# A hybrid decoder step: x loaded ahead of the weights, squares added in pairs, S5 products between the norm's steps

## The chip, the cores and the metric

The kernel runs on one core of a Trainium2 chip. The metric is device microseconds of one execution; lower is better. All data are f32.

## What is computed

One decoder layer over a prompt of 1024 tokens and, beside it, one new token for each of 8 decode sequences whose keys and values (8192 positions) lie in a paged cache.

```
hn = rmsnorm(x, ln1_g)                       # x: 1024 prompt rows + 8 decode rows, 1024 wide
q, k, v, u = split(hn @ w_in)                # 512 columns each
attn = differential attention(rope(q), rope(k), v)     # 4 heads x 2 maps; decode rows read 64 pages of 128 each
s5   = gated S5 state-space group(u)         # 32 groups of 16 channels, 64 complex states
x = x + concat(attn, s5) @ w_out
x = x + hier_moe(rmsnorm(x, ln2_g))          # top-1 of 4 groups, top-2 of 8 experts
y = rmsnorm(x, ln_f_g)
```

lam, which weighs the second attention map, comes from four small vectors (`lamv`) by two dot products and two exponentials.

## The kernel before, in words

Each engine runs its own list of units. The order of the units is written by a small planner (`streams`, `make_plan`): every unit has a TensorE cost and a list of units that must precede it with a lag; the planner puts the streams together by rank, and gives each unit its banks of PSUM (6 banks in turn, `banks`). TensorE, VectorE and GpSimd run the same order `PLAN`; ScalarE runs it sorted by the planned ends. The decode stream has the highest rank. Its unit `K` or `V` multiplies 8 pages of the cache; pages come in a ring of 16 (two units), are sent by the sync queue in a fixed order as slots come free, and the planner paces one unit (2.1 MB) each 7.1 us. Below it stand attention (S, C, T, O), the S5 group (`s5a`, b units), and the projections in halves of 4 of the 8 k slices: `u` (S5 columns transposed, four column blocks n by two token halves a, in parts f), then k, v, q.

Ahead of the planned part three units stand fixed: `stats`, `dqkv`, `dprep`.

- Loads: the sync queue sends, for k = 0 to 7, slice k of x (`xm`) and slice k of the four weight blocks (`w_q, w_k, w_v, w_u`), then the first 16 pages. GpSimd's queue sends consts, colw, rope, br, wr, bglu, lamv and the S5 tables par and bc.
- `stats`: ScalarE squares each slice into one of two buffers `sq`; TensorE sums it over the partitions with a matrix of ones (two products of 512 columns and one of 8 for each slice), VectorE scales the slice by ln1_g (L1025). Then VectorE copies the sums to one row (L1027), TensorE turns the row into columns (18 instructions of one column), VectorE adds eps, GpSimd takes the power -1/2 (L553), VectorE builds 8 diagonals of rstd (L1046).
- `dqkv`: TensorE multiplies the 8 decode rows with all four weight blocks, side by side in four column blocks of the array; ScalarE copies the results (L738), VectorE scales and rotates them.
- `dprep`: TensorE spreads rstd over the partitions (`rep`), transposes the decode queries, keys and S5 inputs (12 transposes, L1805); VectorE writes the queries into `qpad` (32 copies), which the K units read, and the keys into `knT`.
- `lam` runs first of all on VectorE (L1008 to L1017), with one exp on ScalarE.

Matmuls are all recorded at line 1764 (a helper), transposes at L1805 and others.

## Time and profile before

| what | value |
|---|---|
| runs | median 1478.14 us, 1476.67 to 1494.74, 3 runs |
| profiled execution | 1475.24 us |
| its span, first to last instruction | 1473.5 us |
| mean granted TensorE clock | 0.938 |
| busy: TensorE, VectorE, ScalarE, GpSimd | 87%, 35%, 17%, 14% |
| DMA | 458.35 MB, mean 311 GB/s |

The profile shows one execution. Times are in us from the start of the span; the time of an execution is 1.7 us longer than the span here. PE is TensorE, DVE VectorE, ACT ScalarE, POOL GpSimd, SP the sync engine; a trailing q is the engine's sequencer. A matmul of f32 appears as two instructions.

### The profile page before, as it was taken

The page shows a single profiled execution, that of the slowest core. Times are in us where ns is not written, and L with a number is a line of the kernel's source. Part 1 is how long each engine was busy: PE and PEld are TensorE (multiplying, and loading weights), DVE is VectorE, ACT ScalarE, POOL GpSimd, SP SyncE. Part 2 cuts the span into 40 slices and gives each one's busy share as a digit, 9 for nine tenths or more (in the row PEclk, how much of TensorE's full clock was granted, in tenths as well). Part 3 has the DMA queues.
Part 4 walks back from the last instruction along what each step waited for, and adds up shares of the span by engine and source line. Part 5 has one row for each costly group of instructions (what it writes and reads, how often), then busy time and mean ns, then how long its engine had stood idle before and what let it go on. Part 6 is the DMA issues. An engine that isn't in the chain of part 4 may idle for free.

```text
span 1473.5 us, 26489 instructions
## 1 busy us (share of the span) xinstructions
PE 1284.7 (87%) x8952; PEld 670.8 (46%) x8952; DVE 522.2 (35%) x1430; ACT 248.1 (17%) x473; POOL 212.9 (14%) x327
## 2 busy tenths in 40 slices
PE   4799899999889878899869999987799999999930
PEld 2455565654334335566654443433344444444410
DVE  1461344443564555455531121134221121112126
ACT  2200111120122222233321000000111111111111
POOL 1101204040401100000010000000112222222121
PEclk9899999999988989999999999986999999999975
DMA  9499979979987987999996998998899999999754
GB/s 355 173 318 317 340 258 304 344 236 319 313 286 250 366 285 251 368 330 312 325 372 253 337 337 294 314 348 309 284 332 363 368 372 360 367 364 373 259 202 186
DMA packets 186454, 458.35 MB, mean 311 GB/s; under 512 B 24177, under 2 KB 24561, under 8 KB 177778
## 3 DMA queue, kind: packets, MB, share of 16 engines
q1 hardware_dynamic: 165906, 394.41, 75.6%
q0 software_dynamic: 20448, 62.59, 12.7%
q8 instruction: 66, 1.08, 0.3%
q14 instruction: 34, 0.28, 0.1%
HBM read 421.92 MB, written 33.80 MB: 309 GB/s over the span
## 4 chain that ended last, share of the span: by engine, by line
PE 71%; DMA 9%; DVE 8%; SPq 5%; issue 3%; DVEq 2%; ACT 1%; POOL 1%; ACTq 0%; POOLq 0%; PEldq 0%
PE WA L1764 53%; PE SC L1764 7%; PE OD L1764 6%; DMA ring<-in_cacheK 3%; SPq L489 3%; DMA ring<-in_cacheV 2%; PE WA L2110 2%; DMA arena<-in_x_s 1%; SPq L477 1%; PE WA L1865 1%; DVE arena L1733 1%; DVE st L1105 1%; DMA ring<-h_scratch,idc 1%; DMA xm<-in_xT 1%; DVE arena L1746 1%
## 5 line engine op out<-in xcount | busy, mean ns | idle before, releaser
L1764 PE MATMUL WA<-arena 128*128 128x512 f32 (+9 forms) x1440 | 351.8, 428 | 15.3 <-issue 7.1
L1764 PE MATMUL WA<-arena,xm 128*128 128x512 f32 (+2 forms) x768 | 315.7, 619 | 8.7 <-DMA arena<-in_w_out 6.6
L1764 PEld LDWEIGHTS WA<-arena 128*128 128x128 f32 (+2 forms) x1440 | 192.6, 195 | 148.6 <-issue 132.6
L1764 PEld LDWEIGHTS WA<-arena,xm 128*128 128x128 f32 (+1 forms) x768 | 123.5, 182 | 164.1 <-issue 155.9
L1764 PE MATMUL WA<-xm,arena 128*128 128x512 f32 x192 | 88.8, 610 | 1.7 <-ACT arena L936 1.3
L553 POOL TENSOR_TENSOR st<-st,consts 128x1 f32<-128x1 f32 (+2 forms) x18 | 13.8, 765 | 465.5 <-DVEq L1139 279.0
L1764 PE MATMUL OD<-ring,sall 128*32 128x512 f32 x512 | 69.8, 660 | 11.9 <-DMA ring<-in_cacheV 11.9
L1764 PE MATMUL OD<-ring,qpad 128*32 128x128 f32 x2048 | 64.1, 275 | 8.9 <-DMA ring<-in_cacheK 8.7
L1764 PE MATMUL SC<-ring,qpad 128*32 128x128 f32 x2048 | 64.4, 276 | 7.7 <-DMA ring<-in_cacheK 7.5
L1676 DVE TENSOR_TENSOR xm<-WA,colw 128x960 f32<-128x960 f32 x16 | 18.5, 1158 | 147.1 <-PE WA L2110 147.1
L1676 DVE TENSOR_TENSOR arena<-WA,colw 128x960 f32<-128x960 f32 x16 | 18.5, 1158 | 137.5 <-PE WA L2110 137.3
L1764 PEld LDWEIGHTS OD<-ring,qpad 128*32 128x32 f32 x2048 | 53.4, 110 | 28.3 <-issue 16.3
L1764 PEld LDWEIGHTS SC<-ring,qpad 128*32 128x32 f32 x2048 | 54.2, 111 | 26.5 <-issue 16.5
L1764 PE MATMUL SC<-ring,sall 128*32 128x512 f32 x512 | 63.9, 619 | 1.7 <-DMA ring<-in_cacheV 1.7
L804 ACT ACTIVATE arena<-WA,st 128x128 f32<-128x128 f32 (+7 forms) x64 | 47.4, 741 | 94.8 <-DVEq L1109 93.7
L1764 PE MATMUL WA<-ring,xm 128*128 128x512 f32 x128 | 57.5, 603 | 0.0
L671 POOL DMA_DIRECT2D y_dec<-arena x32 | 17.8, 557 | 268.8 <-ACT arena L943 268.8
L1764 PE MATMUL WA<-xm 128*128 128x512 f32 x128 | 56.3, 592 | 0.0
L1764 PEld LDWEIGHTS WA<-xm,arena 128*128 128x128 f32 x192 | 35.7, 194 | 42.1 <-issue 40.5
L943 ACT ACTIVATE arena<-WA 128x1024 f32<-128x1024 f32 x32 | 32.8, 1024 | 125.1 <-PE WA L1764 125.1
L1427 DVE TENSOR_TENSOR arena<-arena,WA 128x512 f32<-128x512 f32 x16 | 11.0, 688 | 113.5 <-PE WA L1764 88.4
L1105 DVE TENSOR_REDUCE st<-WA 128x1 f32<-128x128 f32 (+7 forms) x64 | 48.5, 758 | 5.5 <-issue 0.9
(359 smaller groups left out, 1250.0 us busy)
## 6 DMA issues: line engine op xcount, KB each, us to landing
ring<-in_cacheK SPq DMA_DIRECT2D x512, 256.0 KB, 4.7
ring<-in_cacheV SPq DMA_DIRECT2D x512, 256.0 KB, 4.7
arena<-in_w_gu SPq DMA_DIRECT2D x16, 2048.0 KB, 8.6
arena<-in_w_dn SPq DMA_DIRECT2D x16, 1024.0 KB, 12.5
ring<-in_w_gu SPq DMA_DIRECT2D x8, 2048.0 KB, 8.6
xm<-in_w_gu SPq DMA_DIRECT2D x8, 2048.0 KB, 8.6
arena<-in_w_in SPq DMA_DIRECT2D x32, 256.0 KB, 10.2
ring<-in_w_dn SPq DMA_DIRECT2D x8, 1024.0 KB, 12.6
```

The lines of the kernel that those rows point to most:

```text
L477: sp.dma_start(w[:, k, :], io["w_in"][n, k, :, :]).then_inc(s_wk[k], 16)
L489: sp.dma_start(ring[:, GRP * half + j, :], cache[bass.ds(pages[j], 1), :, :] .rearrange("a p n -> p (a n)")).then_inc(s_pg[PARTS * half + ...
L671: gp.dma_start(io["y_dec"][bass.ds(4 * NB * q + NB * v, NB), :], yb[v % 2][CAP:128, :]).then_inc(m_sd[v % 2], 16)
L804: act.activation(P[:, n % 2, c, 0:w], slot("S", i, h, c)[:, 0:w], ACT.Exp, bias=st[:, 4 * (n % 2) + c:4 * (n % 2) + c + 1], scale=HD ** -0 ...
L943: act.activation(yb[v % 2], W[1][:, :], ACT.Copy).then_inc(m_ys, 1)
L1105: dve.reduce_max(st[:, 8 + c:9 + c], S[:, 0:w], AX)
L1676: dve.tensor_tensor(hgT[v % 2][:, :, 0:CAP], (W[0] if src is None else src)[:, :] .rearrange("p (k n) -> p k n", k=KD)[:, :, 0:CAP], colw[ ...
L1733: dve.scalar_tensor_tensor(x1[0:r, i, :], yg[i][c][0:r, :], wts[0:r, c, i:i + 1], x1[0:r, i, :], MUL, ADD)
L1746: dve.scalar_tensor_tensor(x1[0:r, i, :], x1[0:r, i, :], st[0:r, i:i + 1], lnf[0:r, :], MUL, MUL)\
L1764: return pe.matmul(out, lhsT, rhs, start=first, stop=last, **kw)
L1865: last = pe.transpose(slot("AT", i, h)[:, 128 * j:128 * j + 128], P[:, n % 2, 0, 128 * j:128 * j + 128], ident)
L2110: last = pe.transpose((W[0] if out is None else out)[:, 128 * k:128 * k + CAP], hg[v % 2][0:CAP, 128 * k:128 * k + 128], ident[0:CAP, 0:CAP])
```

## The change

The sync queue sends all of x, then the S5 columns w_u, then the query columns w_q, then pages. w_k and w_v go to GpSimd's queue, sent after `qpad` has been written. GpSimd sends only consts, colw and rope at first; lamv, bglu, br, wr, par and bc follow after the norm's power. ScalarE squares into four buffers, VectorE adds them in pairs (`s_pair`), and TensorE sums over the partitions once for each pair. The fixed head of the order is now: stats, first half of u(0,0), `col` (row to columns), its second half, `dq` (decode queries alone, 128 columns in each of four column blocks), `rep`, first half of u(0,1), `dprep` (4 transposes, 8 copies into qpad, and then `lam`). The decode products of k, v and S5 columns (`dkv`) and their transposes (`dk2`) become units of the projection stream, behind u(3,0). VectorE evacuates u(0,0) after `dprep`. `lam_map` finishes lam at `dkv`.

```diff
-        "stats": [(("ss",), 2)], "dqkv": [(("dp",), 1)], "dprep": [(("rep",), 2), (("dqt",), 1)],
+        "stats": [(("ss",), 2)], "dq": [(("dp",), 1)], "dprep": [(("dqt",), 1)], "rep": [(("rep",), 2)],
+        "dkv": [(("dkv",), 1)], "dk2": [(("dkt",), 1)],
...
-                    dec.append((("K", x, t, g, y), 1.95, [(("ov", SPP * x - 1), 0.8)] if x else []))
+                    dec.append((("K", x, t, g, y), 1.95, [(("ov", SPP * x - 1), 0.8)] if x else [(("dprep",), 0.5)]))
...
     for n in range(4):
         for a in range(2):
             proj += [(("u", n, a, f), half, []) for f in range(2)]
+            if (n, a) == (3, 0):
+                proj.append((("dkv",), 7.5, []))
+    proj.append((("dk2",), 0.9, [(("dkv",), 6.0)]))
...
-    s5 = [(("s5a",), 0.0, [])]
+    s5 = [(("s5a",), 0.0, [(("dprep",), 2.0)])]
     for n in range(NQ):
-        x = [(("bY", n - 1, 1), 0)] if n else [(("u", 3, 1, 1), 4.0), (("s5a",), 60.0)]
+        x = [(("bY", n - 1, 1), 0)] if n else [(("u", 3, 1, 1), 4.0), (("dk2",), 3.0), (("s5a",), 60.0)]
...
-    end, free, nxt = {}, [0.0] * BANKS, 0
-    plan, t = [("stats",), ("dqkv",), ("dprep",)], 0.0
-    land, gone, due = [0.0, 0.0], [], 0.0
+    plan, t = [("stats",), ("u", 0, 0, 0), ("col",), ("u", 0, 0, 1), ("dq",), ("rep",), ("u", 0, 1, 0), ("dprep",)], 0.0
+    end, free = {u: t for u in plan}, [3.0] * BANKS
+    nxt = (max(p + n for p, n, _, _ in [banks(plan)[0][("dqt",)]])) % BANKS
+    at["proj"] = 3
+    land, gone, due = [0.0, 2.0], [], 1.0
     kept, never = {}, 1e9
+    b = banks(plan)[0][("u", 0, 1)][0]
+    free[b], kept[("u", 0, 1, 1)] = never, [b]
...
+    u0, turn = PLAN.index(("u", 0, 0, 1)), PLAN.index(("dprep",)) + 1
+    DVE_PLAN = PLAN[:u0] + PLAN[u0 + 1:turn] + [PLAN[u0]] + PLAN[turn:]
...
-        sq = region(0, 2 * TT, "p (s n) -> p s n", s=2)
+        sq = [region(b, TT) for b in (0, TT, 4096, 4096 + TT)]
...
             for k in range(KD):
                 sp.dma_start(xm[:, k, :], io["xT"][k, :, :]).then_inc(s_xk[k], 16)
-                for n, w in enumerate((w_q, w_k, w_v, w_u)):
-                    sp.dma_start(w[:, k, :], io["w_in"][n, k, :, :]).then_inc(s_wk[k], 16)
+            for k in range(KD):
+                sp.dma_start(w_u[:, k, :], io["w_in"][3, k, :, :]).then_inc(s_wk[k], 16)
+            for k in range(KD):
+                sp.dma_start(w_q[:, k, :], io["w_in"][0, k, :, :]).then_inc(s_wq, 16)
...
-            gp.dma_start(br[:, :], io["b_r"].partition_broadcast(128)).then_inc(s_cst, 16)
-            gp.dma_start(wr[:, :, :], io["w_r"]).then_inc(s_cst, 16)
-            gp.dma_start(bglu[:, :], io["b_glu"]).then_inc(s_cst, 16)
-            gp.dma_start(lamv[:, :, :], io["lamv"].partition_broadcast(128)).then_inc(s_lamv, 16)
-            gp.dma_start(par, io["s5_par"]).then_inc(s_ld5, 16)
-            gp.dma_start(bc, io["s5_bc"]).then_inc(s_ld5, 16)
...
             def stats():
                 gp.memset(qpad[:, :, :, :], 0.0).then_inc(s_qbd, 1)
-                gp.wait_ge(s_cst, 96)
+                gp.wait_ge(s_cst, 48)
                 root(rstd[:, :], ("stats",))
+                gp.dma_start(lamv[:, :, :], io["lamv"].partition_broadcast(128)).then_inc(s_lamv, 16)
+                gp.dma_start(bglu[:, :], io["b_glu"]).then_inc(s_lamv, 16)
+                gp.dma_start(br[:, :], io["b_r"].partition_broadcast(128)).then_inc(s_lamv, 16)
+                gp.dma_start(wr[:, :, :], io["w_r"]).then_inc(s_lamv, 16)
+                gp.dma_start(par, io["s5_par"]).then_inc(s_ld5, 16)
+                gp.dma_start(bc, io["s5_bc"]).then_inc(s_ld5, 16)
...
-            def dqkv():
-                gp.wait_ge(s_drope, 1)
+            def dprep():
+                gp.wait_ge(s_qbd, 2)
+                for n, w in enumerate((w_k, w_v)):
+                    gp.dma_start(w, io["w_in"][n + 1, :, :, :].rearrange("k p n -> p k n")).then_inc(s_wkv, 16)
+
+            def dkv():
+                gp.wait_ge(s_drope, 2)
                 gp.dma_start(io["v_s"], dv[:, :]).then_inc(s_dst, 16)
                 gp.dma_start(io["k_s"], qk[0:NB, QKW:2 * QKW]).then_inc(s_dst, 16)
...
+            def dk2():
+                gp.wait_ge(*filled("dkt"))
...
+                gp.wait_ge(s_qbd, 3)
                 gp.dma_start(io["us_scratch"].rearrange("n p b -> p n b"), usT).then_inc(s_dst, 16)
...
             def stats():
                 for k in range(KD):
                     act.wait_ge(s_xk[k], 16)
-                    if k >= 2:
-                        act.wait_ge(s_sqread, k - 1)
-                    act.activation(sq[:, k % 2, :], xm[:, k, :], ACT.Square).then_inc(s_sq, 1)
-
-            def dqkv():
+                    if k >= 4 and k % 2 == 0:
+                        act.wait_ge(s_sqread, k // 2 - 1)
+                    act.activation(sq[k % 4], xm[:, k, :], ACT.Square).then_inc(s_sq, 1)
+
+            def dq():
                 act.wait_ge(*filled("dp"))
-                for n, out in enumerate((qk[0:NB, 0:QKW], qk[0:NB, QKW:2 * QKW], dv[:, :], du)):
-                    act.activation(out, slot("dp")[32 * n:32 * n + NB, 0:QKW], ACT.Copy)
+                for c in range(4):
+                    act.activation(qk[0:NB, 128 * c:128 * c + 128], slot("dp")[32 * c:32 * c + NB, 0:128], ACT.Copy)
                 act.drain().then_inc(free_sem("dp"), 1)
                 act.drain().then_inc(s_dq, 1)
...
+            def dprep():
+                act.wait_ge(s_lam, 1)
+                act.activation(lamt[:, 2:4], lamt[:, 0:2], ACT.Exp).then_inc(s_lam, 1)
+
+            def dkv():
+                act.wait_ge(*filled("dkv"))
+                for n, out in enumerate((qk[0:NB, QKW:2 * QKW], dv[:, :], du)):
+                    act.activation(out, slot("dkv")[32 * n:32 * n + NB, 0:QKW], ACT.Copy)
+                act.drain().then_inc(free_sem("dkv"), 1)
+                act.drain().then_inc(s_dq, 1)
...
-                    act.wait_ge(*filled("dqt"))
+                    act.wait_ge(*filled("dkt"))
...
             def lam():
-                dve.wait_ge(s_lamv, 16)
+                dve.wait_ge(s_lamv, 64)
...
+
+            def lam_map():
                 dve.wait_ge(s_lam, 2)
...
+                dve.scalar_tensor_tensor(wmap[:, 0:SPP, :].rearrange("p y h -> p (y h)"), consts[:, C_M1:C_M1 + SPP * H],
+                                         lamt[:, 7:8], consts[:, C_M0:C_M0 + SPP * H], MUL, ADD)
+                dve.drain()
 
             def stats():
-                lam()
-                dve.wait_ge(s_cst, 96)
+                dve.memset(rstd[:, NT:NT + 1], 1.0)
+                dve.wait_ge(s_cst, 48)
                 for k in range(KD):
                     dve.wait_ge(s_sq, k + 1)
+                    if k % 2:
+                        dve.tensor_tensor(sq[k % 4 - 1], sq[k % 4 - 1], sq[k % 4], ADD).then_inc(s_pair, 1)
                     dve.tensor_scalar(xm[:, k, :], xm[:, k, :], colw[:, k:k + 1], None, MUL).then_inc(s_xg, 1)
                 dve.wait_ge(*filled("ss"))
                 dve.tensor_copy(sumrow[:, 0:SEQ], slot("ss")[0:1, :])
                 dve.tensor_copy(sumrow[:, SEQ:TT], SC[0:1, 0:NB])
...
-                dve.tensor_scalar(bglu[:, :], bglu[:, :], 0.5, None, MUL)
-                dve.memset(logit[:, NT, :], 0.0)
-                dve.memset(st[:, :], 1.0)
...
                 dve.drain().then_inc(s_rstd, 1)
                 for i in range(NT):
                     dve.tensor_scalar(diag[:, i, :], ident, rstd[:, i:i + 1], None, MUL)
                 dve.drain().then_inc(s_rep, 1)
 
-            def dqkv():
+            def dq():
                 dve.wait_ge(s_dq, 1)
-                r = rstd[0:NB, NT:NT + 1]
-                dve.tensor_scalar(qk[0:NB, :], qk[0:NB, :], r, None, MUL)
-                dve.tensor_scalar(dv[:, :], dv[:, :], r, None, MUL)
-                dve.tensor_scalar(du, du, r, None, MUL)
-                dve.drain()
-                rotate(qk[0:NB, :], NB, NT)
+                dve.tensor_scalar(qk[0:NB, 0:QKW], qk[0:NB, 0:QKW], rstd[0:NB, NT:NT + 1], None, MUL)
+                dve.drain()
+                rotate(qk[0:NB, 0:QKW], NB, NT)
                 dve.drain().then_inc(s_drope, 1)
 
             def dprep():
                 dve.wait_ge(s_qbd, 1)
                 dve.wait_ge(*filled("dqt"))
-                src = slot("dqt")[:, 0:2 * H * NB].rearrange("p (a h b) -> p a h b", a=2, h=H)
+                src = slot("dqt")[:, 0:H * NB].rearrange("p (h x y) -> p h x y", h=H, y=SPP)
                 for h in range(H):
                     for c in range(2):
-                        for y in range(SPP):
-                            dve.tensor_copy(qpad[64 * c:64 * c + 64, h, y::SPP, 8 * y + 2 * h + c],
...
+                        dve.tensor_copy(qpad[64 * c:64 * c + 64, h, :, :].rearrange("p (x y) n -> p x (y n)", y=SPP)
+                                        [:, :, 2 * h + c::40], src[64 * c:64 * c + 64, h, :, :])
                 dve.drain().then_inc(free_sem("dqt"), 1)
+                dve.drain().then_inc(s_qbd, 1)
+                lam()
+                dve.tensor_scalar(bglu[:, :], bglu[:, :], 0.5, None, MUL)
+                dve.memset(logit[:, NT, :], 0.0)
+                dve.memset(st[:, :], 1.0)
+                dve.tensor_scalar(colw[:, 2 * KD:2 * KD + 1], colw[:, 2 * KD:2 * KD + 1], 1.0 - LINIT, None, MUL)
+                dve.drain()
...
+            def dkv():
+                lam_map()
+                dve.wait_ge(s_dq, 2)
+                r = rstd[0:NB, NT:NT + 1]
+                dve.tensor_scalar(qk[0:NB, QKW:2 * QKW], qk[0:NB, QKW:2 * QKW], r, None, MUL)
+                dve.tensor_scalar(dv[:, :], dv[:, :], r, None, MUL)
+                dve.tensor_scalar(du, du, r, None, MUL)
+                dve.drain()
+                rotate(qk[0:NB, QKW:2 * QKW], NB, NT)
+                dve.drain().then_inc(s_drope, 1)
+
+            def dk2():
+                dve.wait_ge(*filled("dkt"))
+                dve.tensor_copy(knT[:, :, :], slot("dkt")[:, 0:H * NB].rearrange("p (h b) -> p h b", h=H))
+                dve.tensor_copy(usT, slot("dkt")[:, H * NB:2 * H * NB].rearrange("p (n b) -> p n b", n=4))
+                dve.drain().then_inc(free_sem("dkt"), 1)
                 dve.drain().then_inc(s_qbd, 1)
...
-            for unit in PLAN:
+            for unit in DVE_PLAN:
...
             def stats():
                 pe.nop().then_inc(s_pgfree, RING // QP)
-                pe.wait_ge(s_cst, 96)
-
-                for k in range(KD):
-                    pe.wait_ge(s_sq, k + 1)
+                pe.wait_ge(s_cst, 48)
+
+                for k in range(KD // 2):
+                    pe.wait_ge(s_pair, k + 1)
                     for out, c0, c1 in ((slot("ss")[:, 0:512], 0, 512), (slot("ss")[:, 512:SEQ], 512, SEQ),
                                         (SC[:, 0:NB], SEQ, TT)):
-                        last = mm(out, ones, sq[:, k % 2, c0:c1], k == 0, k == KD - 1)
+                        last = mm(out, ones, sq[2 * (k % 2)][:, c0:c1], k == 0, k == KD // 2 - 1)
                     last.then_inc(s_sqread, 1)
-                pe.wait_ge(s_sqread, KD)
+                pe.wait_ge(s_sqread, KD // 2)
                 pe.nop().then_inc(full_sem("ss"), 1)
 
+            def dq():
+
+                pe.wait_ge(s_wq, 16 * KD)
+                vacant(pe, "dp")
+                for k in range(KD):
+                    for c in range(4):
+                        last = mm(slot("dp")[32 * c:32 * c + NB, 0:128], xm[:, k, SEQ:TT], w_q[:, k, 128 * c:128 * c + 128],
+                                  k == 0, k == KD - 1)
+                last.then_inc(full_sem("dp"), 1)
+
+            def col():
...
-            def dqkv():
-                pe.wait_ge(s_xg, KD)
-                vacant(pe, "dp")
-                for k in range(KD):
-                    pe.wait_ge(s_wk[k], 64)
-                    for n, w in enumerate((w_q, w_k, w_v, w_u)):
-                        last = mm(slot("dp")[32 * n:32 * n + NB, 0:512], xm[:, k, SEQ:TT], w[:, k, :], k == 0, k == KD - 1)
-                last.then_inc(full_sem("dp"), 1)
-
             def dprep():
+                pe.wait_ge(s_drope, 1)
+                vacant(pe, "dqt")
+                for h in range(H):
+                    last = pe.transpose(slot("dqt")[:, NB * h:NB * h + NB], qk[0:NB, 128 * h:128 * h + 128], ident[0:NB, 0:NB])
+                last.then_inc(full_sem("dqt"), 1)
+
+            def rep_():
                 pe.wait_ge(s_rep, 1)
                 vacant(pe, "rep")
                 for i in range(NT):
                     last = mm(slot("rep")[:, 128 * i:128 * i + 128], ones, diag[:, i, :])
...
-                pe.wait_ge(s_drope, 1)
-                vacant(pe, "dqt")
-                for j in range(3 * H):
-                    src = qk[0:NB, 128 * j:128 * j + 128] if j < 2 * H else du[:, 128 * (j - 2 * H):128 * (j - 2 * H) + 128]
-                    last = pe.transpose(slot("dqt")[:, NB * j:NB * j + NB], src, ident[0:NB, 0:NB])
-                last.then_inc(full_sem("dqt"), 1)
+
+            def dkv():
+                pe.wait_ge(s_wkv, 32)
+                vacant(pe, "dkv")
+                for k in range(KD):
+                    for n, w in enumerate((w_k, w_v, w_u)):
+                        last = mm(slot("dkv")[32 * n:32 * n + NB, 0:512], xm[:, k, SEQ:TT], w[:, k, :], k == 0, k == KD - 1)
+                last.then_inc(full_sem("dkv"), 1)
...
                 if f == 0:
                     vacant(pe, "u", n, a)
                 for k in range(4 * f, 4 * f + 4):
+                    if n + a == 0:
+                        pe.wait_ge(s_xg, k + 1)
+                        pe.wait_ge(s_wk[k], 16)
                     last = mm(slot("u", n, a)[:, :], w_u[:, k, 128 * n:128 * n + 128], xm[:, k, 512 * a:512 * a + 512],
                               k == 0, k == KD - 1)
                 if f == 1:
...
             def m1(x):
                 pe.wait_ge(s_evac, 2 * TURNS * (x + 1))
+                if x == 0:
+                    pe.wait_ge(s_qbd, 3)
```

## Rows read from the trace of the kernel before

**Rows 1.** The page's section 4: the chain that ended last, its shares by engine.

```profile
PE 71%; DMA 9%; DVE 8%; SPq 5%; issue 3%; DVEq 2%; ACT 1%; POOL 1%; ACTq 0%; POOLq 0%; PEldq 0%
```

**Rows 2.** DMA issues from 0 to 60 us: number, KB each, median us from issue to landing.

```profile
xm<-in_xT SPq DMA_DIRECT2D x8, 516.0 KB, 10.6
...
arena<-in_lamv POOLq DMA_DIRECT2D x1, 128.0 KB, 7.6
rope<-in_rope POOLq DMA_DIRECT2D x1, 72.0 KB, 5.6
```

**Rows 3.** Windows: busy us (instructions) by engine, then PEclk, DMA share, GB/s.

```profile
0.00:5.00 5.00, 0.00 (x0) 0.00 (x0) 0.00 (x0) 1.28 (x1) 3.77 (x11) 1.00 0.55 190
...
20.00:25.00 5.00, 5.00 (x15) 2.42 (x14) 1.41 (x2) 1.06 (x1) 0.00 (x0) 1.00 1.04 412
...
50.00:60.00 10.00, 5.84 (x56) 3.21 (x45) 3.25 (x9) 3.60 (x6) 0.61 (x2) 0.89 0.02 7
```

**Rows 4.** Timeline, 0 to 41 us: start, us, engine, line, operation, count, idle time before.

```profile
2.78 0.55 POOL L538 DMA_DIRECT2D rope<-in_rope  x1
...
12.58 0.22 DVE L1008 TENSOR_TENSOR arena<-arena 128x64 f32<-128x64 f32 x1 [12.58 <-DMA arena<-in_lamv]
...
14.72 3.75 PE L1764 MATMUL WA<-arena,consts 128*128 128x512 f32 x4 [14.72 <-ACT arena L733]
...
37.66 1.06 ACT L733 ACTIVATE arena<-xm 128x1032 f32<-128x1032 f32 x1 [2.76 <-DMA xm<-in_xT]
38.76 0.76 DVE L1025 TENSOR_SCALAR xm<-xm,colw 128x1032 f32<-128x1032 f32 x1 [3.07 <-ACT arena L733]
...
38.78 1.98 PE L1764 MATMUL WA<-arena,consts 128*128 128x512 f32 x4 [1.72 <-ACT arena L733]
```

**Rows 5.** Timeline, 41 to 73 us: norm, decode projection, first K unit.

```profile
41.01 1.21 DVE L1027 COPY arena<-WA 1x1024 f32<-1x1024 f32 x1 [1.50 <-PEq L1777]
...
42.38 2.06 PE L1764 MATMUL OD<-consts,arena 1*128 1x1 f32 x18 [1.50 <-DVEq L1029]
...
44.37 8.65 PE L1764 MATMUL WA<-arena,xm 128*8 128x512 f32 x64
...
44.89 1.83 POOL L553 TENSOR_TENSOR rstd<-rstd,consts 128x9 f32<-128x9 f32 x1 [37.38 <-DVEq L980]
...
47.15 1.66 DVE L1046 TENSOR_SCALAR arena<-consts,rstd 128x128 f32<-128x128 f32 x8
...
52.95 2.05 PE L1764 MATMUL WA<-arena,consts 128*128 128x128 f32 x16
...
59.16 1.45 PE L1805 MATMUL WA<-consts,arena 8*128 8x8 f32 x12 [4.16 <-DVEq L1057]
...
60.53 5.75 PE L1764 MATMUL WA<-xm,arena 128*128 128x512 f32 x8
...
66.22 1.95 PE L1764 MATMUL SC<-ring,qpad 128*32 128x128 f32 x64
...
68.10 3.70 PE L1764 MATMUL WA<-xm,arena 128*128 128x512 f32 x8
```

**Rows 6.** Groups of VectorE by form: an SBUF addition or product; busy us, mean ns.

```profile
L1223 DVE TENSOR_TENSOR arena<-arena 128x512 f32<-128x512 f32 x8 | 5.5, 692 | 0.6
```

**Rows 7.** DMA issues from 608 to 640 us.

```profile
arena<-in_w_out POOLq DMA_DIRECT2D x1, 2048.0 KB, 10.4
```

**Rows 8.** TensorE's waits from 608 to 640 us: us in total, times, longest us.

```profile
PE SC L1764 <- DMA ring<-in_cacheK: 2.3, 1, 2.3
```

**Rows 9.** TensorE's waits from 66 to 1000 us: us in total, times, longest.

```profile
PE WA L1865 <- DVEq L1123: 15.3, 8, 5.9
PE OD L1764 <- DMA ring<-in_cacheV: 11.2, 7, 3.6
...
PE OD L1764 <- DMA ring<-in_cacheK: 8.7, 6, 3.3
PE SC L1764 <- DMA ring<-in_cacheK: 7.5, 7, 2.3
```

51 lines of the change are left out of this document (24 added, 27 removed).

## The prediction

> **What bounds the kernel now.** I read the page first: TensorE makes up 71% of the chain that ended last, DMA 9%, VectorE 8%, so TensorE is the bound of the whole [rows 1]. From about 66 us on the kernel is a long queue of TensorE work, in a fixed order, with gaps; what it does before that is a start-up. Then I read the timeline of the first 70 us, because the change touches only that stretch. The reader is to see there a chain of five links.
>
> First, x arrives slowly. The sync queue sends each slice of x (516 KB) followed by four slices of w_in (128x512 f32, 256 KB each) [rows 2], 1,540 KB in all, and the transfers run at 412 GB/s with the DMA engines full [rows 3]: 1.577 MB / 412 GB/s = 3.83 us for each of the eight rounds. The last Square on ScalarE begins at 37.66 and its product on TensorE ends near 40.9 [rows 4]. Second, the norm's small steps: VectorE copies the sums at 41.01, TensorE turns them into columns 42.38 to 44.4, GpSimd takes the power from 44.89 to 46.7, VectorE builds the diagonals from 47.15 to 48.8 [rows 5]. Third, TensorE's decode projection of all four column blocks, 8.65 us from 44.37, then the 16 products for `rep` from 52.95 [rows 5]. Fourth, TensorE stands idle from 55.0 to 59.16 until the copies and the rotation are done, then makes 12 transposes [rows 5]. Fifth, the first half of an S5 product takes 5.75 us where a later one takes 3.70: after that idle time the engine ran it at the low clock for the most part. The first K unit begins at 66.22 [rows 5]. Between 50 and 60 us the DMA engines moved only 7 GB/s [rows 3]: the ring was full and nobody took a page.
>
> **The change, part by part.** I set up the new start-up as a timetable from these rows.
>
> (a) Loads. x goes ahead of all weights, and of GpSimd's transfers only consts, colw and rope stay ahead. Up to 15 us the row of before is not clean (many small packets), so I take its first 5 us (190 GB/s, 0.95 MB) as the start [rows 3] and 410 GB/s from there. x needs 8 x 0.528 = 4.22 MB, the tables 0.54, and about 0.5 MB more has moved when a slice counts as landed (an estimate from before: its last Square, at 37.66, against the bytes ahead of it). The last slice lands at 5 + (5.26 - 0.95)/0.41 = 15.5 us, the S5 columns (2.1 MB) at 20.7, the query columns at 25.8, and the 16 first pages by 36. The rope table, which the gate for VectorE and TensorE now waits for, was issued at 2.78 and took 5.6 us: 8.4 [rows 2, 4].
>
> (b) Squares in pairs. ScalarE: 8 of 1.06 us, from 6.5 on. VectorE does two scalings of 0.76 and one added addition of 128x1032 for each pair; an SBUF addition of 128x512 takes 0.69 [rows 6], and its slope of about 1.04 ns for an element gives 1.23. So 2.75 us a pair. TensorE now makes four sets of products in place of eight: 4 x 2 us saved, of which none lay on the path. The first set runs at the low clock, 3.75 us as before, the others take 2.0 to 2.2 [rows 4]. The timetable: addition 0 ends at 10.4; its products end at 14.1; ScalarE's fifth Square waits for that, since there are four buffers, and ends at 15.2; the sixth at 16.3, addition 2 at 17.5; the seventh Square waits for the second set (16.4 to 17.0), the eighth ends at 19.1; addition 3 at 20.4; the last set at 22.6. The x transfer could be 2 us later without moving this. I take 22.6, with 20.5 (no low clock) and 26 (landing as in the mean of before's first 15 us, and another wait on the table) as its ends. Before it was 40.9.
>
> (c) S5 products between the norm's steps. Now TensorE has work in every gap. From 22.7: half S5 product 3.6, columns 2.1, half 3.6, query projection, `rep` 2.05, half 3.6, 4 transposes 0.5, half 3.6 (no bank is needed, so the planner puts it ahead of the first K unit). The query projection has 64 instructions on 128 columns in four column blocks, the shape of a K unit, 1.95 us [rows 5]; at the low clock it would be 3.9. Sum 22.7 + 3.6 + 2.1 + 3.6 + 1.95 + 2.05 + 3.6 + 0.5 + 3.6 = 43.7 us for the first K unit. The side chains fit under it: the sums are copied by 24.2, before TensorE has ended its half at 26.3; the columns end at 28.4, the power and diagonals follow as before (44.4 to 48.8 is 4.4 us) and are ready at 32.8, while `rep` is needed at 34.0; the queries' copies and rotation take at most what all four blocks took (55.0 minus 52.95 is the time of `rep`, so from 52.95 to 59.16, 6.2 us): from 34.0 to 40.2 against a need at 39.6. At worst 0.6 us shows. The 8 copies into qpad in place of 32 lie beneath the last half. If one of these covers fails the price is that chain's own excess, 1 to 3 us, and if the clock falls during the 2.1 us of columns, one half costs up to 5.75 - 3.6 = 2.2 more [rows 5].
>
> (d) Work moved to later. `dkv` is the old decode projection with three blocks side by side in place of four, still eight steps, and a step on 512 columns is a quarter of 3.6 us: 7.2 us. Its 8 transposes are two thirds of the 1.45 us that 12 took [rows 5]. 8.2 us come back into the TensorE queue. Against it, at the first K unit four S5 halves are done, where before it was one: 3 x 3.6 = 10.8. Net 2.6 more in hand.
>
> (e) w_k and w_v move from the sync queue to GpSimd's and load once qpad is ready (41 us), 4.2 MB or 10.2 us of all DMA engines at 410 GB/s. At first the ring is full and they have the engines alone until page slots come free at 45.7; 2.3 MB are left to run beside the pages. The nearest row is the 2,048 KB of w_out: 10.4 us to land, and TensorE then waited 2.3 us for a page [rows 7, 8]. So 0 to 4.6 us for both; I take 1.5, since half has landed before a page can compete and the next units of K come 12 us later. `dkv` is queued behind some 11 halves, near 90 us, so TensorE won't wait for these weights.
>
> (f) Small loads moved: lamv, b_glu, b_r, w_r behind the power (30.7 us). lamv took 7.6 us [rows 2]; the last of the four was issued at 33 and lands near 41. VectorE waits for all four in `lam`, behind the qpad copies; queued behind that wait are the evacuations of the first two S5 products, whose banks TensorE needs at 45.7. ScalarE's exp is queued ahead of its later copies, and waits for `lam` too. Slack 3 to 4 us, cost nothing; if the loads landed 4 us later each further us would be one on TensorE.
>
> The Trainium skill, "DMA: Bandwidth & Descriptors", section on queues, rings and completion order, says that each DMA engine takes turns between queue rows that have work, a packet at a time. Two busy queues would so get half each, and w_out's row (2.1 MB in 10.4 us, 202 GB/s, half of 410) agrees. By the rule alone the 2.3 MB left in (e) would take 11 us, in which pages are slowed to half: they move 2.3 MB where the planner's pace (2.1 MB in 7.1 us) asks 3.3 MB, so 1.0 MB or 3.5 us late, under the slack of about 4 us, and the sum would lose the 1.5.
>
> **Sum.** TensorE's queue stands 66.2 - 43.7 = 22.5 us earlier at the first K unit and is 2.6 us shorter behind it: 25.1. Less 1.5 for pages: 23.6. The profiled execution took 1475.24 (span 1473.5 and 1.7 around it), so 1451.6. The median of the runs shown is 2.9 higher than that execution and the lowest 1.4 higher; I add 1: 1452. From 20.5 and 26 for the start, 0 to 4.6 for pages and 0 to 2.8 for clock and covers, the likeliest case spans 1446 to 1459.
>
> **The rivals.** A: the pages bound it. The gain of the TensorE queue is then cut by the weights that now load beside pages. Before, with the ring full at 66.2, all of w_in was in; after, with the ring full at 43.7, 2.3 MB are still to come when pages start again: 22.5 - 5.7 = 17, so 1459. For it: DMA engines are full in many slices, and waits of TensorE for pages sum to 27 us over 66 to 1000 [rows 9]. Against it: that is a small part of 934 us, so TensorE is the bound and pages only touch it.
>
> B: more comes back. The written order is made anew from other starting values, other banks and one longer stream, and the waits inside the attention stage (15.3 us on one line of VectorE alone) and for pages are matters of which units meet [rows 9]. These sum to 43 us. If a fifth falls away it is 9 us more: 1443. Nothing in the rows says that it does, and a fifth more of them is as possible: 1461.
>
> C, on the other side: the new order bunches K and V units so that the ring of two units runs dry. A wait of that kind was 3.6 us at its longest [rows 9], so seven more of that size take 25 us, the whole gain, and eight end slower than before, at 1480 against 1478. It decides from the point where the page waits double, from 27 to 51 us. Against it: the pace of pages in the planner is not changed.
>
> D: a cover in (f) fails. GpSimd sends lamv's group from 30.7 on, while VectorE works through diagonals, copies and rotations until 41; before, it sent it to an idle VectorE, whose first instruction is at 12.58 [rows 4], so no row here tests the two together. If those loads get going only when VectorE rests, they land at 41 + 7.6 = 48.6, VectorE frees the first S5 bank at 50, and TensorE, which wants it at 45.7, loses 4.3 us: 1456. That w_k and w_v go the same way costs nothing, with 40 us to spare. The Trainium skill, "SBUF — State Buffer" (section on SBUF's two separate sides), has such a rule: a transfer issued from GpSimd can't have its descriptors written while VectorE runs an instruction in a two-port mode. That VectorE is in that mode for only part of the ten us is why I give it little.
>
> **Chances.** Forecast 0.52, A 0.15, B 0.12 for more and 0.10 for less, C 0.03, D 0.08. The range 1441 to 1463 leaves out 0.15 to 0.2. The bound of 2%, about what a measurement of this kernel can tell from no change, lies at 1448.6 against the median of 1478.14: below it is B's better half and the lower edge of the forecast, 0.12 + 0.16 = 0.28. Above 1507.7 there is a part of C, 0.02. The rest, 0.70, is within 2%.
>
> **What would show it.** In the profile after: the last Square near 18 to 19 us; no gap of TensorE over 1 us between 23 and 44 us; the first K unit at 41 to 47; the clock granted at full from 15 us on; idle DMA only between some 36 and 41 us; the decode products of k, v and S5 near 90 us, 7.2 us long. Then each later landmark (first V unit, the routing) should lie 22 to 28 us earlier. I am wrong if landmarks drift apart after 100 us, which would be order or pages, or if the first K unit lies beyond 48, which would be the start-up.

## The result, and the profile after

The changed kernel took 1465.72 us (median of 8 runs, 1459.21 to 1472.42), the kernel before 1480.12 (median of 8 in all, the three shown first among them, 1475.01 to 1494.74). The ratio is 0.9898, 95% interval 0.9871 to 0.9924: 1.0% faster, 15.1 us on 1480.12, between 11.2 and 19.1. The forecast was 1452, its range 1441 to 1463: too low, and the range misses. The profiled execution after took 1465.81 (span 1464.1), its own median; that of before, 1475.24, turned out to lie 4.9 under its median.

The chain that ended last, from the page of the kernel after, answers to [rows 1]:

```profile
PE 70%; DMA 9%; DVE 7%; SPq 5%; issue 3%; DVEq 2%; ACT 1%; POOL 0%; ACTq 0%; POOLq 0%
```

TensorE is still the bound. The timeline of the kernel after (start, length, engine, line, operation, count, idle time before) answers to [rows 4, 5]:

```profile
8.57 0.76 DVE L1059 TENSOR_SCALAR xm<-xm,colw 128x1032 f32<-128x1032 f32 x1 [7.59 <-DMA rope<-in_rope]
...
10.61 3.75 PE L1807 MATMUL WA<-arena,consts 128*128 128x512 f32 x4 [10.61 <-DVE arena L1058]
...
14.69 2.02 ACT L751 ACTIVATE arena<-xm 128x1032 f32<-128x1032 f32 x2 [3.58 <-PE SC L1807]
...
16.91 2.02 ACT L751 ACTIVATE arena<-xm 128x1032 f32<-128x1032 f32 x2 [0.20 <-PE SC L1807]
...
20.51 1.98 PE L1807 MATMUL WA<-arena,consts 128*128 128x512 f32 x4 [0.37 <-DVE arena L1058]
...
22.92 3.67 PE L1807 MATMUL WA<-xm,arena 128*128 128x512 f32 x8 [0.30 <-PE SC L1807]
...
26.52 2.06 PE L1807 MATMUL OD<-consts,arena 1*128 1x1 f32 x18
...
28.51 5.40 PE L1807 MATMUL WA<-xm,arena 128*128 128x512 f32 x8
...
33.84 1.93 PE L1807 MATMUL WA<-arena,xm 128*8 128x128 f32 x64
...
35.70 2.05 PE L1807 MATMUL WA<-arena,consts 128*128 128x128 f32 x16
...
37.59 3.60 PE L1807 MATMUL WA<-xm,arena 128*128 128x512 f32 x8
...
41.12 0.41 PE L1844 MATMUL WA<-consts,arena 8*128 8x8 f32 x4
...
41.46 3.70 PE L1807 MATMUL WA<-xm,arena 128*128 128x512 f32 x8
...
43.51 1.80 POOL L578 DMA_DIRECT2D arena<-in_w_in x2 [9.41 <-DVEq L1090]
...
45.09 1.96 PE L1807 MATMUL SC<-ring,qpad 128*32 128x128 f32 x64
...
60.78 1.08 PE L1807 MATMUL SC<-ring,qpad 128*32 128x128 f32 x32 [1.15 <-DMA ring<-in_cacheK]
66.07 1.94 PE L1807 MATMUL SC<-ring,qpad 128*32 128x128 f32 x32 [4.21 <-DMA ring<-in_cacheK]
67.93 4.53 PE L1807 MATMUL WA<-xm,arena 128*128 128x512 f32 x8
...
81.57 1.63 PE L1807 MATMUL OD<-ring,qpad 128*32 128x128 f32 x52
```

The reader is to see three things. From 22.9 to 45 us TensorE goes from one item to the next with no gap, and the first K unit begins at 45.09, where before it was 66.22 [rows 5]. The two loads of w_k and w_v are issued at 43.5, 1.6 us ahead of that unit. And the third K unit waits for pages twice, 1.15 and 4.21 us. The windows of the kernel after show the DMA side of it (busy us by engine, then PEclk, DMA share, GB/s):

```profile
37.00:44.00 7.00, 7.00 (x25) 3.49 (x25) 3.56 (x19) 1.02 (x1) 0.49 (x1) 1.00 0.18 71
44.00:50.00 6.00, 6.00 (x74) 3.31 (x73) 4.43 (x17) 0.31 (x2) 1.89 (x3) 1.00 0.73 234
50.00:60.00 10.00, 9.62 (x82) 4.64 (x80) 5.54 (x41) 3.23 (x5) 0.00 (x0) 1.00 1.03 366
60.00:67.00 7.00, 2.01 (x52) 1.69 (x56) 5.78 (x44) 0.00 (x0) 0.00 (x0) 0.70 1.04 405
67.00:72.00 5.00, 5.00 (x28) 2.31 (x20) 4.26 (x31) 0.00 (x0) 0.00 (x0) 0.74 1.05 386
```

The DMA engines rest at a share of 0.18 from 37 to 44 us and are full from 50 on. From 60 to 67 TensorE works 2.0 of 7 us and its mean granted clock falls to 0.70. In single windows it is at its lower level, 0.50, from 62.9 to 69.6 us, after TensorE had waited since 61.9. So the second half of the K unit takes 1.94 us in place of 1.08, and the S5 half behind it 4.53 in place of 3.7. That makes the price of the stall: the fifth K unit, which before came at 95.4, comes at 81.6, 13.8 us earlier, while the first came 21.1 earlier. 7.3 us are lost between the two: 5.4 waits for pages, most of the rest the low clock behind them.

TensorE's waits over 45 to 1000 us in the kernel after (total, times, longest) answer to [rows 9]:

```profile
PE WA L1930 <- DVEq L1166: 15.8, 4, 11.1
PE OD L1807 <- DMA ring<-in_cacheK: 15.3, 9, 4.9
PE OD L1807 <- DMA ring<-in_cacheV: 15.2, 7, 5.4
PE SC L1807 <- DMA ring<-in_cacheK: 11.6, 6, 4.2
PE WA L1948 <- DVEq L1188: 7.4, 5, 3.3
```

The page waits of these rows sum to 42.1 us against 27.4 for the same three kinds before [rows 9]: 14.7 more, 5.4 of them the third K unit; the other 9.3 lie behind it. Landmarks further on: issue of the first expert weights at 1003.93 against 1015.73, 11.8 earlier; end, by the two profiled executions, 9.4 earlier, by the medians 14.4.

### The profile page after: what moved, and what is told of

Its sections match the earlier page's. It is cut to its first block, busy times and chain, and to the rows that moved or that the text cites. A ratio compares the mean times of both kernels' runs of the same rounds, so it can differ in the third digit from the quotient of the medians.

```text
span 1464.1 us, 26527 instructions
## 1 busy us (share of the span) xinstructions
PE 1275.4 (87%) x8976; PEld 669.1 (46%) x8976; DVE 525.6 (36%) x1417; ACT 248.3 (17%) x476; POOL 214.7 (15%) x329
## 3 DMA queue, kind: packets, MB, share of 16 engines
q0 software_dynamic: 21504, 66.78, 13.5%
q8 instruction: 66, 1.08, 0.3%
## 4 chain that ended last, share of the span: by engine, by line
PE 70%; DMA 9%; DVE 7%; SPq 5%; issue 3%; DVEq 2%; ACT 1%; POOL 0%; ACTq 0%; POOLq 0%
PE WA L1807 52%; PE OD L1807 7%; PE SC L1807 6%; DMA ring<-in_cacheK 5%; SPq L503 5%; DMA ring<-in_cacheV 2%; PE WA L2177 2%; PE WA L1930 1%; DVE arena L1776 1%; DMA ring<-h_scratch,idc 1%; DVE arena L1789 1%; DVE st L1148 1%; PE WA L2137 1%; DMA arena<-y_scratch 1%; DVEq L1778 1%
## 5 line engine op out<-in xcount | busy, mean ns | idle before, releaser
L1807 PE MATMUL WA<-arena 128*128 128x512 f32 (+10 forms) x1440 | 350.9, 430 | 16.6 <-issue 7.2
L1807 PE MATMUL WA<-arena,xm 128*128 128x512 f32 (+3 forms) x816 | 313.4, 580 | 7.2 <-DMA arena<-in_w_out 5.3
L1807 PE MATMUL OD<-ring,sall 128*32 128x512 f32 x512 | 71.0, 671 | 15.4 <-DMA ring<-in_cacheV 15.2
L566 POOL TENSOR_TENSOR st<-st,consts 128x1 f32<-128x1 f32 (+2 forms) x18 | 13.8, 765 | 469.5 <-DVEq L1182 280.4
L1807 PE MATMUL OD<-ring,qpad 128*32 128x128 f32 x2048 | 67.8, 285 | 15.3 <-DMA ring<-in_cacheK 15.3
L1807 PEld LDWEIGHTS OD<-ring,qpad 128*32 128x32 f32 x2048 | 56.5, 114 | 35.1 <-DMA ring<-in_cacheK 18.3
L970 ACT ACTIVATE arena<-WA 128x1024 f32<-128x1024 f32 x32 | 32.7, 1023 | 125.2 <-PE WA L1807 125.2
```

The costliest lines, as they stand in the source:

```text
L970: act.activation(yb[v % 2], W[1][:, :], ACT.Copy).then_inc(m_ys, 1)
L1807: return pe.matmul(out, lhsT, rhs, start=first, stop=last, **kw)
```

## Experiments

Each was timed beside the kernel before on the same chip, in five rounds; times are medians, ratios are to the kernel before with 95% intervals. "Old order" is the list of units that the planner makes in the kernel before, "new order" that of the kernel after.

**1. w_k and w_v issued in the idle DMA window.**

```diff
             def stats():
...
                 gp.dma_start(bc, io["s5_bc"]).then_inc(s_ld5, 16)
+                for n, w in enumerate((w_k, w_v)):
+                    gp.dma_start(w, io["w_in"][n + 1, :, :, :].rearrange("k p n -> p k n")).then_inc(s_wkv, 16)
...
-            def dprep():
-                gp.wait_ge(s_qbd, 2)
-                for n, w in enumerate((w_k, w_v)):
-                    gp.dma_start(w, io["w_in"][n + 1, :, :, :].rearrange("k p n -> p k n")).then_inc(s_wkv, 16)
```

> Theory (the load of w_k and w_v beside the pages cost the changed kernel 7 us: waits of 1.15 and 4.21 us at the third K unit and the low clock behind them): sent 10 us earlier, while the ring is full and the engines idle, these waits go, the fifth K unit begins 6 to 7 us earlier than in the changed kernel, and the time falls from about 1466 to 1459. Rival 1 (the order written by the planner lost it): the third K unit's wait goes, but the time stays within 3 us of 1466, since other units wait instead. Rival 2 (pages bound the kernel, any 4 MB more costs its share wherever it is): no wait at the third K unit, page waits later grow by as much, time 1464 to 1467.

1458.57 us, ratio 0.9836 (0.9793 to 0.9879). Timeline and windows of this kernel:

```profile
34.12 1.82 POOL L564 DMA_DIRECT2D arena<-in_w_in  x2
...
45.12 1.95 PE L1804 MATMUL SC<-ring,qpad 128*32 128x128 f32 x64
...
59.58 1.96 PE L1804 MATMUL SC<-ring,qpad 128*32 128x128 f32 x64
...
74.27 1.95 PE L1804 MATMUL OD<-ring,qpad 128*32 128x128 f32 x64
```

```profile
37.00:44.00 7.00, 7.00 (x26) 3.52 (x25) 3.57 (x19) 1.02 (x1) 0.00 (x0) 1.00 1.00 397
44.00:50.00 6.00, 6.00 (x74) 3.31 (x73) 4.44 (x17) 0.31 (x2) 0.58 (x1) 1.00 1.02 412
```

The first K unit stays where it was (45.12), the idle window is full (397 GB/s in place of 71), no unit up to the fifth waits for a page, and the fifth comes at 74.27: 7.3 us before the changed kernel's. So it is the loads' time of issue that cost 7.3 us up to there.

How much of it reaches the end is less sure. The medians of the two kernels lie 7.2 us apart, on two chips, and the intervals of their ratios touch (0.9836, up to 0.9879, against 0.9898, from 0.9871). By the two profiled executions the end comes 5.2 us earlier, and the page waits over 45 to 1000 us are no fewer than the changed kernel's 42.1:

```profile
PE OD L1804 <- DMA ring<-in_cacheK: 17.9, 10, 3.7
PE OD L1804 <- DMA ring<-in_cacheV: 17.8, 10, 6.3
...
PE SC L1804 <- DMA ring<-in_cacheK: 7.0, 6, 1.7
```

They sum to 42.7. The half of rival 2 that speaks of waits (they grow elsewhere by as much) came true in this profile; its time, 1464 to 1467, did not.

**1b. The same kernel again**, on another chip beside experiment 7.

> The early kernel once more, to see how far its time holds and beside the kernel with eight buffers on the same chip. Theory: 23.7 us of start-up lead and no load beside the pages, 1456 to 1459, ratio to the kernel before 0.983 to 0.986. Rival (its first time was a lucky one and the load costs less than 7 us): 1462 and above.

1459.29 us, ratio 0.9859 (0.9833 to 0.9886). The time holds to within 1 us, below the expectation's rival (1462 and above); this interval too touches the changed kernel's. Its page waits sum to 42.9 us, and its profiled execution ends 5.7 us before the changed kernel's.

**2. One load at a time.** w_k goes out behind the first S5 stage's u store, w_v behind the second's; they were issued at 46.6 and 80.8 us.

```diff
                     gp.dma_start(io["u_scratch"][n, :, :, :], ustage[n % 2]).then_inc(s_ust[n % 2], 16)
+                    if n < 2:
+                        w = (w_k, w_v)[n]
+                        gp.dma_start(w, io["w_in"][n + 1, :, :, :].rearrange("k p n -> p k n")).then_inc(s_wkv, 16)
```

> w_k is sent only after the first column block of S5 products is out and w_v after the second, so that each 2 MB competes with pages in a running stream, with 10 us or more between them. Theory: pages have some 4 us of slack each time, so each load costs 0 to 2.3 us, like w_out before: the page waits between 50 and 100 us sum to 1 to 4 us against 5.4, and the time is 1461 to 1465. Rival 1 (order): no change of the time beyond 2 us. Rival 2 (4 MB cost their share anywhere): waits of 5 to 7 us in sum, time 1465 to 1467.

1465.84 us, ratio 0.9901 (0.9869 to 0.9933), as the changed kernel and as rival 2 had it. Page waits from 50 to 110 us were 3.1 and 2.8 us, 5.9 in sum. The low clock behind each comes on top: the S5 halves there took 5.02 and 5.36 us in place of 3.70. From the first K unit (43.51) to the decode products (104.58) this kernel needs 61.1 us, experiment 1 needs 51.4 (45.12 to 96.53) and the changed kernel 58.7. So each load of 2 MB beside the pages cost some 5 us here, and one at a time cost no less than both together.

**3. The same loads from ScalarE's queue**, at the same point (issued at 44.15).

```diff
                 act.activation(lamt[:, 2:4], lamt[:, 0:2], ACT.Exp).then_inc(s_lam, 1)
+                act.wait_ge(s_qbd, 2)
+                for n, w in enumerate((w_k, w_v)):
+                    act.dma_start(w, io["w_in"][n + 1, :, :, :].rearrange("k p n -> p k n")).then_inc(s_wkv, 16)
```

> The changed kernel with w_k and w_v sent from ScalarE's queue in place of GpSimd's, at the same point: behind the exp of lam, near 44.4 us. In the changed kernel, from 47 to 59 us, while both kinds of load were queued, GpSimd's queue moved 3.34 MB in 831 packets (4.0 KB each) and the sync queue, which carries the pages, 0.97 MB in 523 packets (1.9 KB each). Theory 1, it matters whose queue carries the weights: the pages fell behind because GpSimd's queue takes the larger packets and so three quarters of the bytes. From ScalarE's queue both kinds of packet are alike, the pages get about half, some 2 MB in those 12 us, TensorE's page waits at the third K unit (5.4 us) fall under 2 us, and the fifth K unit begins 3 to 5 us earlier than the 81.6 of the changed kernel, so the time falls to some 1461 to 1463. Theory 2, only the bytes count: 4.2 MB stand ahead of the pages wherever they are sent from, the waits up to the fifth K unit stay at 5 to 6 us, and the time stays at the changed kernel's 1465.7.

1462.07 us, ratio 0.9865 (0.9832 to 0.9899). Queues from 47 to 59 us (packets, MB, share of the 16 engines) in the changed kernel, then in this one; q1 carries the pages, q0 GpSimd's loads and the u store, q10 ScalarE's:

```profile
q0 software_dynamic: 831, 3.34, 79.2%
q1 hardware_dynamic: 523, 0.97, 22.1%
...
ring<-in_cacheK SPq DMA_DIRECT2D x13, 256.0 KB, 14.1
```

```profile
q10 hardware_dynamic: 1301, 2.63, 61.7%
q1 hardware_dynamic: 699, 1.29, 28.8%
q0 software_dynamic: 144, 0.52, 10.7%
```

The pages got 1.29 MB instead of 0.97, not the 2 MB of theory 1, though the packets of both queues are now alike (2.0 and 1.8 KB). One wait of 3.7 us replaced the 5.4, between the two theories, and the fifth K unit came at 80.87, 0.7 earlier where theory 1 had 3 to 5. So theory 2 is nearer, and in both kernels the weight loads took twice what the pages got or more. The median lies in theory 1's range, but 1462 against 1465.7 can't be told apart by these intervals.

Two loads side by side are not needed for such a split. In experiment 2 one load took 2.18 MB while the pages got 1.25 (82 to 92 us). And in the kernel before, from 615 to 624 us, while w_out loaded [rows 7]:

```profile
q0 software_dynamic: 144, 2.10, 60.0%
q1 hardware_dynamic: 722, 1.32, 39.3%
```

**4. Squares not in pairs**: the changed kernel with every Square sent to TensorE, from the same four buffers.

```diff
-                    if k % 2:
-                        dve.tensor_tensor(sq[k % 4 - 1], sq[k % 4 - 1], sq[k % 4], ADD).then_inc(s_pair, 1)
...
-                for k in range(KD // 2):
-                    pe.wait_ge(s_pair, k + 1)
+                for k in range(KD):
+                    pe.wait_ge(s_sq, k + 1)
```

> The squares go to TensorE one by one, from the four buffers. Theory: TensorE then does 8 sets of 2.2 us, the first at the low clock (3.9): from the first Square behind the gate (8.6) that is 8.6 + 3.9 + 0.9 + 7 x 2.2 = 28 at the latest, against 22.6, if TensorE is the bound; so the first K unit comes at about 49 to 50 in place of 45.1, 4 to 5 us later, and the time is about 1470. Rival: ScalarE and x are the bound, TensorE keeps up, and the pairs were worth under 2 us: first K unit by 47, time 1466.

1469.80 us, ratio 0.9919 (0.9889 to 0.9949). The last sum's products end at 27.0 in place of 22.6, back to back at 1.94 us a set: with x this early, eight sets are TensorE's bound. The first K unit begins at 47.83 (2.7 later, the S5 half behind the columns took 3.70 here). The pairs are worth 4.4 us at the last sum; in the median 4.1, which the intervals can't tell from nothing. Without them the rest of the gain stays: 47.83 against 66.22 in the kernel before.

**5. The order.** In the kernel before only the planner's starting values were changed (banks free at 3, pages landed at 2, S5 chain behind the decode preparation); the start-up is that of before.

```diff
-    s5 = [(("s5a",), 0.0, [])]
+    s5 = [(("s5a",), 0.0, [(("dprep",), 2.0)])]
...
-    end, free, nxt = {}, [0.0] * BANKS, 0
-    land, gone, due = [0.0, 0.0], [], 0.0
+    end, free, nxt = {u: t for u in plan}, [3.0] * BANKS, 0
+    land, gone, due = [0.0, 2.0], [], 1.0
```

> The kernel before, with nothing changed but the planner's starting values (those of the changed kernel), so the start-up is the same and only the order after 66 us is another. Theory (order is a small term): within 3 us of the kernel before, 1477 to 1483, first K unit within 2 us of where the order puts it. Rival 1 (order moves the time by ten us): 1470 or 1490, with the page and VectorE waits from 66 to 1000 us changed by as much.

1509.51 us, ratio 1.0198 (1.0165 to 1.0231). The first K unit began at 66.19, as before, but the S5 half that stood ahead of it now stands behind it, and TensorE waited 3.86 us for the copies into qpad: at the fifth K unit (97.24 against 95.36) it is 1.9 us late with one half of 3.6 us less done. So some 5.5 of the 28 us are start-up, and this run is not the order behind it alone. TensorE's waits from 66 to 1000 us in this kernel:

```profile
PE WA L1883 <- DVEq L1145: 19.0, 5, 6.8
PE OD L1764 <- DMA ring<-in_cacheK: 16.9, 10, 5.1
PE WA L1764 <- issue: 10.0, 7, 3.2
PE WA L1931 <- ACTq L839: 8.4, 1, 8.4
```

One of them, 8.4 us for ScalarE's sequencer, has nothing like it in the kernel before, whose longest wait of that kind is 1.2. Starting values alone move this kernel by 28 us, some 23 of them behind the start-up; which waits make these up was not taken apart. So start-up and order were crossed:

```diff
-    order, ends = make_plan()
+    order, ends = [u for u, _ in ORDER], dict(ORDER)   # ORDER: the other kernel's list, slot by slot
```

The changed kernel's start-up with the old order:

> The changed kernel with its own start-up, but behind it the units follow the list of the kernel before, slot by slot (the decode products take the places of the S5 halves that are done by then). Theory (start-up 23.7, minus 7.2 for the weights beside the pages, and the rest, about 2 us in the medians, is the new order): 1463 to 1468, as the changed kernel. Rival (the new order costs much more or much less, as an order alone moved the kernel before by 28 us): with the old order the changed kernel comes to 1455 or below, the waits between 100 and 1000 us as in the kernel before.

1466.85 us, ratio 0.9907 (0.9872 to 0.9941).

The kernel before with the new order:

> The kernel before with its own start-up, but behind it the list of the changed kernel, slot by slot. Theory (the new order is worth -2 to +2): 1479 to 1484. Rival (the new order costs 8 us or more by itself): 1488 and above. It should give the same sign and size as the old order in the changed kernel.

1489.24 us, ratio 1.0065 (1.0038 to 1.0091). The three kinds of page waits sum to 38.4 us here (16.0, 11.2 and 11.2) and to 35.9 in the one above (14.1, 11.0 and 10.8), between 27.4 for old with old and 42.1 for new with new. These are single executions, and the one with 38.4 took 1496.81 us, the slowest of its twelve. That both the list and the start-up raise the waits is likely by them, and not shown.

Experiment 1 with the old order:

> The kernel with w_k and w_v sent early, and the list of the kernel before behind its start-up: if load and order add up, its time is that of the early kernel (1458.6) plus what the old order does to the changed kernel. If the whole gain of the start-up arrives with the old order, 1456 to 1458 (1480 less 23.7); rival: waits move about so much with any shift that the two don't add up within 4 us.

1462.28 us, ratio 0.9869 (0.9829 to 0.9909).

The new order costs 9.5 us on the old start-up and nothing that can be measured on the new one: 1.1 us the other way by the medians, 3.7 the other way with the loads sent early. Effects of order don't add to those of the start-up.

**6. x first, nothing else**: the kernel before with all slices of x ahead of all weights on the sync queue.

```diff
                 sp.dma_start(xm[:, k, :], io["xT"][k, :, :]).then_inc(s_xk[k], 16)
+            for k in range(KD):
                 for n, w in enumerate((w_q, w_k, w_v, w_u)):
```

> The kernel before, with only the sync queue's order changed: all of x, then the rounds of four weight slices. The last Square then comes near 20 to 24 in place of 37.7 (TensorE's eight sets of 2.2 us, the first at the low clock), the weights are all there by 38 as before (same bytes), the decode projection ends near 39 in place of 52.95, and the first K unit begins near 52 to 53. Theory (the order is the same, so the lead of the start-up arrives whole): 13 to 14 us faster than before, 1466 to 1468, i.e. two lines bring as much as the whole change. Rival (something else holds the later stages back, pages above all, since the 16 first pages now lie only 5 us ahead of the first K unit): 1472 or more.

1473.92 us, ratio 0.995 (0.9925 to 0.9976). Timeline:

```profile
14.48 0.20 ACT L921 ACTIVATE lamt<-lamt 128x2 f32<-128x2 f32 x1 [12.36 <-DVEq L1014]
14.59 2.00 ACT L734 ACTIVATE arena<-xm 128x1032 f32<-128x1032 f32 x2
...
37.56 8.75 PE L1765 MATMUL WA<-arena,xm 128*8 128x512 f32 x64
...
59.83 1.95 PE L1765 MATMUL SC<-ring,qpad 128*32 128x128 f32 x64
```

In the changed kernel the first Square ran at 4.80; here it stood behind lam's exp on ScalarE, whose data (lamv) landed at 13.6; then TensorE's eight sets ran back to back. So x's place alone gives 6.4 us at the first K unit, and 5.8 in the median; the 13 to 14 expected are missed at the start-up itself, and the rival's number (1472 or more) came true for another cause than the pages. That lamv must come late for x early to pay is read from this timeline; no run moves lamv alone. By the medians the lead of 6.4 arrived, in an unchanged order. The two profiled executions don't show it: that of this kernel, 1479.71, lies 5.8 above its median, and ends 4.5 after that of the kernel before.

**7. Experiment 1 with eight square buffers and rope off the first gate.**

```diff
-        sq = [region(b, TT) for b in (0, TT, 4096, 4096 + TT)]
+        sq = [region(b, TT) for b in (0, TT, 4096, 4096 + TT, 13312, 13312 + TT, 13312 + 2 * TT, 4096 + 2 * TT)]
...
-            gp.dma_start(rope[:, :, :], io["rope"]).then_inc(s_cst, 16)
+            gp.dma_start(rope[:, :, :], io["rope"]).then_inc(s_rope, 16)
```

> The early kernel, with a buffer for each square, so that ScalarE never waits for TensorE, and with the rope table off the gate of VectorE and TensorE. In the early kernel ScalarE idled 3.6 us for the first products, at the low clock, and the gate opened at 8.57. Theory: VectorE is then the bound of the sums, four pairs of 2.75 us from about 7.5 us on, so the last sum's products end at 20 to 21 in place of 22.6, the first K unit begins at 42.5 to 43.5, and the time is 2 us below the early kernel, some 1456. Rival (at this size the waits behind it move more than the start-up): start-up as said, but the time is anywhere within 4 us of the early kernel, above it too.

1456.01 us, ratio 0.9846 (0.9822 to 0.987), the lowest median of all. Timeline:

```profile
18.67 1.96 PE L1803 MATMUL WA<-arena,consts 128*128 128x512 f32 x4
...
26.66 3.70 PE L1803 MATMUL WA<-xm,arena 128*128 128x512 f32 x8
...
41.54 1.95 PE L1803 MATMUL SC<-ring,qpad 128*32 128x128 f32 x64
```

The sums end at 20.7 in place of 22.6, the half behind the columns took 3.70 in place of 5.40, and the first K unit came at 41.54, 3.6 us before experiment 1's. Some 1.5 of these are the faster half, which 1b had too, without this change: against 1b (43.63) it is 2.1. The median is 3.3 under that of 1b, and the intervals can't tell the two apart.

## Why the prediction was wrong, step by step

**What bounds the kernel, and the start-up (a to d, f): right, up to the clock.** Last Square forecast for 18 to 19 us, begun at 17.9; last sum 22.6, measured 22.6; no gap of TensorE over 1 us between 23 and 44; first K unit 43.7, measured 45.1. The 1.4 are the S5 half behind the columns, 1.8 us longer than 3.6: the granted clock was 0.50 from 28.7 to 32.1 us, against the sign "at full from 15 us on". This was named as a bound (up to 2.2) and not in the sum. Experiment 2, with 3.70 there, had its first K unit at 43.51. The first set of products took 3.75 us as forecast, but the profile's granted clock reads 1.00 there (10.6 to 14.4 us): the time is shown, its name "low clock" is not. The products of step (d) took 7.23 us (7.2 forecast), at 103.8 and not near 90, which cost nothing. So 21.1 + 2.6 = 23.7 us were in hand at the first K unit, against 25.1.

**Step (e), w_k and w_v beside the pages: mis-sized. This is the step that failed.** Forecast 1.5 us, at most 4.6; measured 7.3 at the fifth K unit, by the timeline and by experiment 1, which takes it away there. Two of its grounds failed. I gave the loads a head start of 4.7 us (41 to 45.7), in which "they have the engines alone"; they were issued at 43.5 and 44.4, since the eight copies into qpad ended at 43.1, the DMA engines moved nothing before 45 us, and the next page was issued at 46.4. And I took half of the DMA time for the pages; from 47 to 59 they got 0.97 of 4.34 MB. That the clock falls behind a page wait (1.8 us here) was in no term, though the kernel before has it behind the 2.3 us of [rows 8]: its granted clock is 0.83 from 620 to 630 us. Rival A had the mechanism (weights beside the pages cut the gain, 17 us left, chance 0.15), and 23.7 - 7.3 = 16.4 is near its number. That is in part luck: it reckoned with 2.3 MB left beside the pages where all 4.2 were, and left out the 2.6 us of step (d). I gave the forecast more than three times its chance.

The Trainium skill, "DMA: Bandwidth & Descriptors", section on queues, rings and completion order, has each engine take turns between queue rows by packets. I read that as half of the bytes each. The trace disagrees with the reading: by packets 523 of 1,356, by bytes 22%, and with like packets 29% (experiment 3). Nor does w_out's row agree, though the prediction says so: its 202 GB/s are half of 410, but the pages beside it got 1.32 of 3.41 MB, 39%. What sets this split no run settles.

**The base.** The sum was made against the profiled execution, 1475.24, with 1 us added; the median of eight runs was 4.9 above it. That is 3.9 of the miss.

The miss of 13.7 us is thus: 1.4 start-up, 5.8 pages, 3.9 base, 0.6 rounding down to 1452, and 2.0 left over, inside the interval of the ratio (11.2 to 19.1 us gained, against 16.4). This sum takes it that the 7.3 reach the end, which the medians of experiment 1 bear out and its profile only in part. One sum of the prediction is off besides: its own terms (20.5 to 26 for the start, 0 to 4.6, 0 to 2.8) span 1448 to 1461 around 1452, not 1446 to 1459.

**Rival B, order: too small.** I gave it 9 us either way; the new order cost 9.5 on the old start-up, and starting values alone moved the kernel before by 28, some 23 of them order (experiment 5). That the two orders at hand differ by about 1 us on the new start-up is luck: nothing in the prediction led to it.

**Rival C** (pages wait twice as much, slower than before): the page waits rose by half, 27.4 to 42.1 us, and its point of 51 was not reached. The landmarks did drift after 100 us, the sign named for order or pages: 13.8 us of lead at the fifth K unit, where step (d) should add 2.6, and 11.8 at the expert weights. Experiments 1 and 1b keep as many page waits without the loads, so most of the rise has another cause than step (e); which one no run settles. **Rival D** (lamv's group late): it did not happen. lam's first instruction on VectorE ran at 43.31, right behind the qpad copies, with no wait for a load; lamv had landed 5.4 us after its issue. The Trainium skill, "SBUF — State Buffer", section on SBUF's two separate sides, has the rule that spoke for it; this trace shows no harm from it, with the loads issued at 30.8 to 33.0 and needed ten us later. It is a weak trial: VectorE worked from 31.0 to 32.7 and then not before 37.1.

## What to carry to other kernels

Put a moved bulk load into the window in which the DMA engines rest, not at the first point where a ring starts to drain: beside a ring of two units each 2 MB cost 3.7 to 5 us, the low clock behind the waits included, and there is no head start unless the instruction that it waits for has really ended. Cost a start-up change at the first item of the steady queue and follow its lead from landmark to landmark; what is lost between two of them has a place. A wait taken away can come back elsewhere, so look at the later waits and at the end too. Where a planner writes the order, hold its list fixed while you judge another change, since its starting values alone can move more than the change does.
